# ScalarE's high parts one turn later, first in their turn, and norms ahead of inner tiles: the five seams of a transformer block

## The reference

```
for l in range(DEPTH):                      # DEPTH = 2
    f = swiglu(modulate(x, sh1, sc1), ffn_in[l, 0], ffn_out[l, 0])
    x = deepnorm_residual(x, f, g1, ln_g[l, 0], ln_b[l, 0], 0.5)
    u = modulate(x, sh2, sc2)
    m = even_mixer(u, ...) if l % 2 == 0 else odd_mixer(u, ...)
    x = deepnorm_residual(x, m, g2, ln_g[l, 1], ln_b[l, 1])
    f = swiglu(modulate(x, sh3, sc3), ffn_in[l, 1], ffn_out[l, 1])
    x = deepnorm_residual(x, f, g3, ln_g[l, 2], ln_b[l, 2], 0.5)

def deepnorm_residual(x, f, gate, g, b, weight=1.0):
    return layer_norm(DN_ALPHA * x + weight * (1 + gate[:, None, :]) * f, g, b)
def modulate(x, shift, scale):
    return x * (1 + scale[:, None, :]) + shift[:, None, :]
def swiglu(u, w_in, w_out):
    gate, up = jnp.split(u @ w_in, 2, axis=-1)
    return (jax.nn.silu(gate) * up) @ w_out
```

## Time and profile before

| | |
|---|---|
| median of 3 runs | 4109.48 us (4103.06 to 4112.79) |
| the profiled execution | 4102.35 us, its span 4101.1 us |
| TensorE busy | 3783.1 us, 92% of the span |
| VectorE, ScalarE, GpSimd busy | 55%, 37%, 28% |
| mean granted clock of TensorE | 0.962 of full speed |

### The profile page before, as it was taken

The page is one execution under the profiler, slowest core; times in us unless marked ns, Lnnn a source line. Parts: engine busy times, 40 slices in busy tenths (PEclk is TensorE's granted clock), DMA queues, the critical chain, the costliest instruction groups (busy, mean ns, idle before and its releaser), DMA issues.

```text
span 4101.1 us, 54103 instructions
## 1 busy us (share of the span) xinstructions
PE 3783.1 (92%) x21364; PEld 3142.0 (77%) x21364; DVE 2245.6 (55%) x3735; ACT 1499.0 (37%) x2546; POOL 1133.2 (28%) x755
## 2 busy tenths in 40 slices
PE   5999899989998999798999799899999989899999
PEld 4888768788888888657888677678877867678777
DVE  6555684576656777645433689831156238840352
ACT  3223553443234323344322322442235223453352
POOL 1102204242015102204201423913221334525224
PEclk8999999999999999899999999899999999999999
DMA  7565324235654554303332311002110112113112
GB/s 265 175 199 158 124 75 157 91 130 185 227 179 133 186 194 160 100 31 109 127 99 83 122 48 55 33 27 72 49 49 12 65 49 77 48 36 106 60 37 93
DMA packets 131595, 433.12 MB, mean 106 GB/s; under 512 B 14480, under 2 KB 14480, under 8 KB 130704
## 3 DMA queue, kind: packets, MB, share of 16 engines
q1 hardware_dynamic: 130912, 427.04, 31.3%
q10 hardware_dynamic: 432, 2.62, 0.2%
HBM read 427.51 MB, written 2.10 MB: 105 GB/s over the span
## 4 chain that ended last, share of the span: by engine, by line
PE 73%; DVE 16%; issue 4%; ACT 4%; POOL 1%; DMA 1%; SPq 0%; DVEq 0%; ACTq 0%; POOLq 0%
PE ps L610 20%; PE ps L611 20%; PE ps L612 20%; DVE cut L2129 6%; PE ps L1847 2%; DVE cut L1033 1%; PE ps L1731 1%; PE ps L1814 1%; PE ps L1824 1%; ACT cut L528 1%; PE ps L608 1%; ACT cut L1869 1%; PE ps L636 1%; PE ps L637 1%; PE ps L638 1%
## 5 line engine op out<-in xcount | busy, mean ns | idle before, releaser
L610 PE MATMUL ps<-cut 128*128 128x512 f32 (+1 forms) x5216 | 1872.7, 359 | 160.3 <-DVE cut L538 45.7
L611 PE MATMUL ps<-cut 128*128 128x512 f32 (+1 forms) x5216 | 1835.2, 352 | 0.0
L612 PE MATMUL ps<-cut 128*128 128x512 f32 (+1 forms) x5216 | 1833.7, 352 | 0.0
L610 PEld LDWEIGHTS ps<-cut 128*128 128x128 f32 x5216 | 1012.4, 194 | 319.4 <-issue 99.2
L611 PEld LDWEIGHTS ps<-cut 128*128 128x128 f32 x5216 | 1014.0, 194 | 129.8 <-issue 4.8
L612 PEld LDWEIGHTS ps<-cut 128*128 128x128 f32 x5216 | 1012.1, 194 | 126.0
L538 POOL TENSOR_TENSOR cut<-cut 128x1024 fp32r<-128x1024 f32 (+3 forms) x304 | 671.1, 2211 | 1262.8 <-ACT cut L528 1262.2
L528 ACT ACTIVATE cut<-cut 128x1024 fp32r<-128x1024 f32 (+3 forms) x680 | 631.5, 936 | 532.5 <-PE ps L612 456.6
L538 DVE TENSOR_TENSOR cut<-cut 128x1024 fp32r<-128x1024 f32 (+3 forms) x376 | 447.8, 1193 | 458.6 <-ACT cut L528 458.5
L879 POOL TENSOR_TENSOR cut<-cut 128x512 fp32r<-128x512 f32 (+1 forms) x100 | 137.1, 1371 | 1011.2 <-ACT cut L839 1011.2
L2129 DVE SCALAR_TENSOR_TENSOR cut<-cut,cols 128x512 f32<-128x512 f32 (+1 forms) x330 | 280.4, 850 | 11.7
(11 more groups left out here) (293 smaller groups left out, 3901.3 us busy)
## 6 DMA issues: line engine op xcount, KB each, us to landing
cut<-in_ffn_in SPq DMA_DIRECT2D x200, 512.0 KB, 4.0
cut<-in_mod_w SPq DMA_DIRECT2D x128, 512.0 KB, 4.3
cut<-in_ffn_out SPq DMA_DIRECT2D x96, 384.0 KB, 3.2
cut<-in_ffn_out SPq DMA_DIRECT2D x96, 320.0 KB, 3.0
cut<-in_w_ada SPq DMA_DIRECT2D x48, 512.0 KB, 3.5
cut<-in_w_merge SPq DMA_DIRECT2D x48, 512.0 KB, 3.5
cut<-in_even_in SPq DMA_DIRECT2D x36, 512.0 KB, 3.6
cut<-in_proj SPq DMA_DIRECT2D x48, 256.0 KB, 2.6
```

Of the source, the lines that this page charges most:

```text
L610: te.matmul(o, hi[:, k - ka, w], xs[0], start=k == 0, stop=False)
L611: te.matmul(o, hi[:, k - ka, w], xs[1], start=False, stop=False)
L612: ins = te.matmul(o, lo[:, k - ka, w], xs[0], start=False, stop=last)
```

## The change

It edits the orders of ScalarE and VectorE at the seams, and no operation, operand or size.

1. `act_ln(m)` no longer makes the high parts of tiles 2m and 2m+1, but those of tiles 2m-2 and 2m-1. Where the norm has only turns 0 to 3 (S1's and S4's second halves, `last` is 3), turn 3 makes tiles 4 to 7.
2. In `act_tail` the high parts stand ahead of the turn's square, in turns from 1 on.
3. In feed forwards ScalarE makes them ahead of the turn's silu or inner tile, and VectorE runs `dve_ln(m)` ahead of its inner tile's product.

```
 act_ffn epilogue(m):
                     x = FTMP[(tile0 + m // 2) % 2][:, g[0]:g[1]]
+                    if gu[-1] == "A" and m:
+                        yield from act_ln(u, "B", m)
                     se.wait_ge(*(yield ("p_mm", gu, m) if m % 2 == 0 else ("v_hid", gu, m)))
...
-                    if gu[-1] == "A":
-                        yield from act_ln(u, "B", m)
+                    if gu[-1] == "A" and m == 0:
+                        yield from act_ln(u, "B", 0)
 dve_ffn epilogue(m):
+                    if gu[-1] == "A":
+                        yield from dve_ln(u, "B", m)
                     if m % 2:
...
-                    if gu[-1] == "A":
-                        yield from dve_ln(u, "B", m)
 act_tail epilogue(m):
+                if part[-1] == "B" and m:
+                    yield from act_ln(tag, "A", m)
                 yield from act_square(part, tag, m)
-                if part[-1] == "B":
-                    yield from act_ln(tag, "A", m)
+                if part[-1] == "B" and m == 0:
+                    yield from act_ln(tag, "A", 0)
 act_ln:
-    def act_ln(tag, h, m):
+    def act_ln(tag, h, m, last=4):
...
-        for t in (2 * m, 2 * m + 1) if m < 4 and tag != "f11" else ():
+        for t in range(2 * m - 2, 8 if m == last else 2 * m) if 0 < m <= last and tag != "f11" else ():
 act_rg (twice) and act_odd: the call gets last=3
-                    yield from act_ln("f00", "B", 2 * t)
+                    yield from act_ln("f00", "B", 2 * t, 3)
```

More of the change, by code:

```diff
@@ L1181, in act_rg @@
                 if x == "A":
-                    yield from act_ln("f00", "B", 2 * t)
+                    yield from act_ln("f00", "B", 2 * t, 3)
                 yield from act_linear(("ga", t, x), nothing)
                 if x == "A":
-                    yield from act_ln("f00", "B", 2 * t + 1)
+                    yield from act_ln("f00", "B", 2 * t + 1, 3)
         for t in range(2, NT):
@@ L1631, in epilogue @@
                 if name[-1] == "A":
-                    yield from act_ln("f10", "B", m)
+                    yield from act_ln("f10", "B", m, 3)
             yield from act_linear(name, epilogue)
```

## The result

The changed kernel takes 4079.89 us (median of four runs, 4077.31 to 4088.97), the kernel before 4108.55 us in the same rounds. The ratio is 0.9935, 95% interval 0.9915 to 0.9955.

A forecast was written before the change was run, and what follows sets the result against it. TensorE, busy 92% of the span, was taken as the bound, with only its waits and slow-clock stretches winnable. Gains in tails, next products and feed forwards summed to 10.2 us, giving 4099 us from the median; range 4084 to 4110.

The forecast's parts named there:

- the sum for the tails: Five tails: 2.6 us in S1, 1.9 in S4, 0.5 in S3, 1.5 in S2, 0 in S5; together 6.5 us.
- the schedule of turns 1 to 3: S1's tail: VectorE's and GpSimd's work summed as before; squares 1.2 and 0.1 us sooner, group 4's 1.9 us sooner.
- 0.7 us more: S1's tail: a wait cut from 3.73 to about 1.8 us shortens the slow-clock stretch behind it by 0.7 us.
- Turn 0 of S1: S1's tail: GpSimd's early low part delays VectorE about 0.9 us; turn 0 ends at 403.2, the square at 404.85.
- the order in which the two get the lock: VectorE and GpSimd at their shared SBUF port: the order, taken from one tail, is where the forecast fails first.
- the work of the two adds up: Seams: VectorE's SBUF instructions stand still while GpSimd works, so their times must be added, not overlaid.
- S3's tail: Two GpSimd low parts push turn 0 back by over 2 us; 0.5 us of the removed wait is left.
- The order inside a turn: Tails: squares stand behind two high parts, 1.09 us later in ScalarE's turn, costed at nothing.
- Next products and feed forwards: Next products win 2.25 us in S4, 0.5 in S1; feed forwards win 1.2 in S2, lose 0.3 in S3, S5 nothing.
- S5's tail: GpSimd's low part moves ahead of the residual in three turns and pays back what it wins: 0 us.
- the second: Rival: GpSimd's low parts fit gaps, long waits fall under a microsecond, clock stays up; 26 us, 4083 us; chance 0.18.
- The rival with a slower kernel by the lock in the mean's chain: Ten norms: GpSimd's low part falls on the reciprocal's successors, up to 2 us each; +10 us net, 4119; chance 0.12.

The follow-up runs named there:

- e6_v_lows: The changed kernel with all low parts of the slabs in the tails' half B on VectorE, none on GpSimd: 4072.03 us, 6.6 us faster than the changed kernel.
- e5_behind_square: The changed kernel with the tails' high parts behind the square of their turn, not ahead of it: 4097.12 us, 18.5 us slower than the changed kernel.
- c2_changed: The changed kernel run and profiled once more, nothing edited: 4078.59 us against 4101.41 us before, ratio 0.9949.

## Why the prediction was wrong

**The failed step is the sum for the tails, 6.5 us where 15.9 were won.** In S1, which the other tails were read from, two terms of it were too small: the schedule of turns 1 to 3, where the squares come "1.2 us and 0.1 us sooner than before" and at last 1.9 us (3.0, 1.3 and 3.6 us sooner at TensorE), and the "0.7 us more" for the clock (measured 2.6). Direction, places and the first turn were right. By my own steps:

- *Turn 0 of S1 was right.* The tail starts 0.63 us sooner in the changed trace. On its clock I had turn 0 end at 402.6 and the square at 404.2; measured 402.35 and 403.94. GpSimd's low part at 398.24 lies under the reciprocal and stretches one instruction, L1054, from 0.42 to 1.12 us: 0.7 us for the 0.9 that I charged. S3's turn 0 is pushed back by 2.1 us, as forecast (reciprocal's end to L913: 4.4 us in place of 2.4).
- *Turns 1 to 4 were too long, the term that was mis-sized.* On that clock I had the squares of groups 2, 3 and 4 end at 410.8, 416.8 and 423.4; they ended at 408.94, 415.63 and 421.36. I had put both of GpSimd's low parts, at full length, ahead of the residual of group 2. Three things make it less. GpSimd's total at 403.56 takes 2.53 us in place of 0.74, because it is held off while six instructions of VectorE, L1038 to L1066, run at full speed: GpSimd pays there, not VectorE. Only one low part (406.05 to 407.94) then falls ahead of the residual, on the second L1075. And the residual slips in between the two low parts at its normal 0.47 us. I had named the order in which the two get the lock as the point where the forecast fails first. For S1 the VectorE term is 421.65 against 425.87, less 0.63, so 3.6 us, where I had 1.9; the second profile, with its wait of 1.34 us, gives 3.6 too.
- *That the work of the two adds up was not the error.* From the residual of group 1 to that of group 4 VectorE takes 19.23 us before (405.66 to 424.89), of which 1.54 us are the wait for a slab, and 17.42 us after (403.01 to 420.43), each time with four of GpSimd's low parts. So it is 17.7 us of work and stretching before and 17.4 after. e6_v_lows, which takes GpSimd's low parts away, needs 15.3. If the sum stays, what turn 0 has won must stay as well; my schedule lost it on the way, from 1.7 us at the first square to 0.1 at the third.
- *The clock term was mis-sized as well.* I had 0.7 us for a shorter slow stretch, read from a group behind a wait of 1.77 us. In fact the slow stretch behind that square's wait went wholly, 6.70 us to 4.38. S1's tail won 6.2 us, so 2.6 are left for the clock, 2.3 of them in this group. The experiment behind the square, where VectorE won 0.3 us and the clock 2.5, shows this part by itself. S4 has the same pattern (5.1 us, against 1.9, granted clock of its tail 0.89 and 1.00): up to the square of group 4 it won 3.6 us (its wait ends 31.4 us after the tail's start before and 27.8 after), and 1.5 behind it. I had left the clock out of S2 and S3.
- *S3's tail* is the largest miss for its size, 3.6 us for 0.5. Turn 0 is pushed back by 2.1 us as I said, and the first square comes 1.1 us later (10.20 us after the tail's start before, 11.29 after). But the third comes 2.0 us sooner (24.85, then 22.85), where I had 0.5 left for the whole tail, and the group behind it takes 5.02 us in place of 5.97, at the faster clock.
- *What a faster clock gives depends on the place.* In S1's tail TensorE was busy 37.0 us in the first and 35.8 us in the second profile of the changed kernel, and the tail was 41.7 and 41.8 us long: ahead of a wait for VectorE, slow matmuls cost nothing. Only the stretch behind the last wait counts.
- *The order inside a turn was right.* I costed the high parts ahead of the square at nothing. They are no cost but the gain itself: the other way round the kernel is 18.5 us slower.
- *Next products and feed forwards* came close: 3.3 us for 2.75, and 2.4 for 0.9, with the wait of 2.00 us where I had put 2.1. What I did not ask was whether this half of the edit should be made at all; without it the feed forwards win 8.4 us more.
- *S5's tail*, 0 forecast, lost 0.7 us: GpSimd's low parts come ahead of the residual there, as said.

Of the rivals, the second ("more is won", 4083 us) comes nearest to the outcome, in the time and in part of the mechanism: the granted clock of S1's tail rose from 0.89 to 0.96 and 1.00 in the two profiles, but the long waits fell to 2.8 us and not under one, and the clock still fell behind some of them. Its argument against, that VectorE has few gaps, didn't hold: it was idle for 6.2 of 34.6 us there, and the window that answers to the first of the earlier trace rows has it idle for 1.1 us (busy for 27.31 of 28.40) and is 6.2 us shorter. On the tail's clock the residual of group 4 comes 3.8 us sooner in it, and 3.07 of them are the two waits for slabs: what I had given as a bound, that they go and nothing refills them, is what came in S1.

```profile
393.77:422.17 28.40, 24.52 (x178) 23.60 (x178) 27.31 (x47) 14.81 (x25) 17.08 (x11) 0.94 0.39 121
```

The rival with a slower kernel by the lock in the mean's chain did not come; that price is 0.7 us in S1 and 2.1 in S3.

What stays open: mixer 1. The changed kernel's first profile won 4.3 us there, its second lost 0.6, with the same instructions. TensorE's busy time in it is 372.3 us before, 369.3 in the first profile and 372.9 in the second, so most of it is the clock. Of the 14 traces of this case five, of four different kernels, have 4.2 to 4.4 us won there, and no other has more than 1.4; why the clock falls in one and not in the other no run shows.

## What to carry to other kernels

When two engines hold each other up, the sum of their work can be right over several turns (17.7 and 17.4 us here) and the forecast still wrong: find in the timeline which instruction stands behind which, and carry what one turn has won through to the next. A low part that GpSimd makes in 1.8 us can cost VectorE more than the 0.8 to 0.95 us of making it itself; moving such work to the engine that is "fully busy" won 7 and some 20 us here.

An order is best tested edit by edit: of four moved pieces one (VectorE's norm ahead of its inner tile) cost 8 to 10 us of what the others won. And in an in-order queue, put ahead of a waiting instruction whatever the engine that it waits for needs next.

A stretch at half clock behind a long wait is a cost of its own (2.3 us of 6.70), to be booked apart from the wait, and only where no later wait absorbs it.

## What the runs showed of the hardware

**A run of VectorE instructions can hold GpSimd off, but doesn't always.** In e6_v_lows GpSimd's total takes 2.53 us three times, while six VectorE instructions with two SBUF operands run at their normal length:

```profile
404.74 2.53 POOL L980 TENSOR_TENSOR cut<-cut 128x256 f32<-128x256 f32 x1 [12.15 <-DVE cut L913]
409.82 2.53 POOL L980 TENSOR_TENSOR cut<-cut 128x256 f32<-128x256 f32 x1 [2.56 <-DVE cut L913]
414.91 2.53 POOL L980 TENSOR_TENSOR cut<-cut 128x256 f32<-128x256 f32 x1 [2.55 <-DVE cut L913]
```

The same total takes 0.72 us where VectorE is idle (e5_behind_square, 403.48). GpSimd got through each of the three times at the change from L1066 to the scalings L1075. The Trainium skill ("SBUF — State Buffer", the part on the two sides of the SBUF's ports) has the lock go to whoever starts first, for the whole instruction. The scaling that stood 1.93 us (406.16, the second of the pair at 405.41) agrees. That five borders between instructions of VectorE let nobody in goes beyond what it says for one.

It is no rule, though. A total of the changed kernel (S3's tail) and one of the kernel before (S1's) start as far into the first of six such instructions, 0.16 us, and get in at the first border:

```profile
1251.62 0.86 POOL L980 TENSOR_TENSOR cut<-cut 128x256 f32<-128x256 f32 x1 [1.49 <-DVE cut L913]
```

```profile
406.21 0.84 POOL L976 TENSOR_TENSOR cut<-cut 128x256 f32<-128x256 f32 x1 [1.15 <-DVE cut L911]
```

Then VectorE pays: its next instruction takes 0.95 us in place of 0.41. Of the 13 totals that start so, with five more two-operand instructions to come, in the tails of the changed kernel's first profile, nine take 2.5 us and four 0.84 to 0.86; in the kernel before all five take 0.83 to 0.84. The same instruction of the same kernel took 2.52 us in one profile (415.26) and 0.84 in the other (c2_changed, 416.22). What decides it no run shows.

**The clock does not answer the same wait the same way.** In mixer 1 TensorE waits 1.68 us at the same instruction in both traces, before and after:

```profile
620.76 0.50 PE L610 MATMUL ps<-cut 128*128 128x512 f32 x1 [1.68 <-ACT cut L1398]
```

```profile
613.37 0.50 PE L610 MATMUL ps<-cut 128*128 128x512 f32 x1 [1.68 <-ACT cut L1403]
```

Windows of the two stretches (busy PE, then the other engines, and granted clock), before and after:

```profile
620.76:626.50 5.74, 5.74 (x18) 3.45 (x19) 3.56 (x7) 1.37 (x2) 3.16 (x1) 0.96 0.86 280
626.50:633.50 7.00, 7.00 (x28) 5.26 (x27) 3.41 (x5) 2.32 (x3) 3.10 (x1) 0.54 0.36 119
```

```profile
613.40:619.40 6.00, 6.00 (x19) 3.55 (x20) 3.81 (x7) 1.56 (x3) 3.13 (x1) 1.00 0.83 287
619.40:626.40 7.00, 7.00 (x55) 6.44 (x54) 3.13 (x5) 2.46 (x4) 3.21 (x1) 1.00 0.38 126
```

In the same 7 us TensorE did 28 matmuls at a mean clock of 0.54, most of it at 1.2 GHz, and 55 at 2.4 GHz. The same instruction waits in all 14 traces (1.68 us in 13, 2.02 in one): in five of them the clock stays up behind it, in nine it falls within 8 us. The two profiles of the changed kernel are one of each kind. Single profiles of this kernel so carry up to 5 us at one place that belong to no edit.
